# Matrix products that read and write in runs of 32 columns, alternating between the two halves of their columns

## The chip, the cores and the metric

The kernel runs on one NeuronCore of a Trainium2 chip. The metric is device time in microseconds (us) of one execution, start to end, and the time of a kernel is the median of several executions. Besides the times there is one profiled execution of the kernel before, from which all rows below are taken.

## What is computed

One block of a bidirectional encoder on 512 tokens of width 2048, in float32. A normed input is projected to 10,304 columns, which feed two attention branches of eight heads each: a differential one (two softmaxes, subtracted) and one with compressed queries, keys and values. Both are gated and merged, and one more product and a norm end the block. Cut to what matters:

```python
h = _rmsnorm(x, norm_g[layer])
proj = h @ w_in[layer]
aq, ak, av, ag, cq, ckv, kr, bg, mg = jnp.split(proj, SPLIT_POINTS, axis=-1)
...
oa = _diff_attention(aq[..., 0, :], aq[..., 1, :], ak[..., 0, :], ak[..., 1, :], av, pos_f, lam, slopes)
oa = _rmsnorm(oa, a_subln_g[layer], SUBLN_EPS) * (1.0 - lam_init)
ya = (oa.reshape(b, s, A_WIDTH) * jax.nn.silu(ag)) @ w_oa[layer]

q = (_rmsnorm(cq, q_norm_g[layer]) @ w_uq[layer]).reshape(b, s, B_HEADS, B_NOPE + B_ROPE)
kv = (_rmsnorm(ckv, kv_norm_g[layer]) @ w_ukv[layer]).reshape(b, s, B_HEADS, B_NOPE + B_V_DIM)
...
ob = _mla_attention(q_nope, q_rope, k_nope, k_rope, vb)
yb = (ob.reshape(b, s, B_WIDTH) * jax.nn.silu(bg)) @ w_ob[layer]

ga, gb = jnp.split(mg, 2, axis=-1)
merged = jax.nn.sigmoid(ga) * ya + jax.nn.sigmoid(gb) * yb
x = x + merged @ w_out[layer]
return _rmsnorm(x, final_g)
```

## The kernel before

**Numbers in two parts.** Every float32 operand of a large product is split into a high part, rounded to the format `float32r`, and a low part that holds the rest. `three` (L2113) makes one product of two such operands out of three TensorE instructions into the same bank of PSUM: high by high, high by low, low by high. Each of these instructions has a stationary operand of 128 x 128 words, loaded by a LDWEIGHTS of its own, and a moving operand of 128 partitions by 512 columns (256 columns in `pv`, L2183). Its result is 128 partitions by as many columns, and fills a whole bank of PSUM (2 KB in each partition) or half of one.

**Stages.** The program on TensorE is one stream, written out by hand. It begins with `WARM_UP` products of the identity and the transposes of the normed input (`turn_unit`, L2200). Then come 92 merge steps and what belongs to them (`merge_product`, L2289): the compressed columns, the values and the merge gates, the last two with Strassen's seven products in place of eight (`product`, L2236, with its sums `s12` and `s34`). Then eight heads of the first branch (`a_head`, L2426, with `project`, `scores_a`, `turn_p_a`, `pv` and `feature_sums`), eight of the second (`b_up`, `b_gate`, `scores_b`), the two products of the branches (`y_block`, L2582), and the last product (`merge_product` again, and a loop over `three` at the end, L2645 to L2660). `rotary_keys` (L2463) has products with a result of 64 partitions among its own.

**Operands.** Where a moving operand is a weight of a merge step, `hi_of` and `lo_of` hand it over as two blocks of 256 columns, `[P, 2, 256]`. In most steps the two blocks lie side by side, so that the instruction reads 512 words in one piece. In the steps whose raw data went into one of the two shared slots (`st.raw >= OWN_RAW`, in `blocks`, L478) the low part lies in the upper halves of rows of another tile, and the two blocks are 512 words apart: the instruction reads 256 words, jumps, and reads 256 more. The names `duo<-h_hi,s_hi`, `duo<-h_lo,s_hi`, `duo<-h_lo,h_hi` and `duo<-h_hi` at L2116 in the rows below are these steps; the first name after the arrow is the moving operand. All other moving operands and all results are one piece of consecutive words:

```python
own = o_hi[st.hi] if st.n >= OUT0 else m_hi[:, st.hi, :]
return own[:, p0 * SEQ:p1 * SEQ].rearrange("p (a b) -> p a b", b=HALF_T)
```

**Other engines.** ScalarE rounds the high parts, VectorE subtracts to get the low ones, SyncE starts the loads, and both compute engines read the banks when a group of products is complete. `duo` is the name of PSUM in the rows: four tensors of two banks each.

Of the kernel before, what the change touches and what calls it, by code (L numbers as in the profile page):

```python
# [27 lines left out]
KT = D_MODEL // P  # L28
# [8 lines left out]
LAM_INIT = 0.8 - 0.6 * math.exp(-0.3 * 0)  # L37
SLOPE0, SLOPE_RATIO = 2.0 ** (-8.0 / HEADS), 2.0 ** (-8.0 / HEADS)
NORM_EPS, SUBLN_EPS = 1e-6, 1e-5


SLOTS = 4
# [186 lines left out]
def hybrid_encoder(nc, x, positions, norm_g, w_in, lam_q1, lam_k1, lam_q2, lam_k2, a_subln_g, w_oa,  # L229
                   q_norm_g, w_uq, kv_norm_g, w_ukv, w_ob, w_out, final_g, consts, out):  # L230
    ctx = ExitStack()
    with ctx:
# [3 lines left out]
        def at(name, kb, shape, dt=F32):  # L236
            return nc.alloc_sbuf_tensor_at(name, shape, dt, offset=base + int(kb * KB))

        def sem(name):
            return ctx.enter_context(nc.semaphore(name))  # L240


        h_hi = at("h_hi", 0, [P, KT, SEQ], F32R)
        h_lo = at("h_lo", 32, [P, KT, SEQ], F32R)
# [62 lines left out]
        start = at("start", 96, [P, TOK, SEQ])  # L307
# [6 lines left out]
        q_hl = at("q_hl", 160, [P, 2, SEQ], F32R)  # L314
        k_hl = at("k_hl", 164, [P, 2, SEQ], F32R)


        qa = at("qa", 160, [P, 2, SEQ], F32R)
        ka = at("ka", 164, [P, 2, SEQ], F32R)
        ka_lo = at("ka_lo", 198, [P, 2, SEQ], F32R)  # L320
        vT = at("vT", 168, [P, SEQ])
        vT_lo = at("vT_lo", 168, [P, SEQ], F32R)
        vT_hi = at("vT_hi", 142, [P, SEQ], F32R)
# [12 lines left out]
        kr_hi = at("kr_hi", 198, [P, SEQ], F32R)  # L336
        kr_lo = at("kr_lo", 200, [P, SEQ], F32R)
        qr_hl = at("qr_hl", 202, [P, SEQ], F32R)
        v_raw = at("v_raw", 202, [P, TOK, P])
        ones_sq = at("ones_sq", 204, [P, P], F32R)  # L340
# [47 lines left out]
        ACC = bank[0:2]  # L388
        SC = bank[2:6]
        TR = bank[6]  # L390
# [44 lines left out]
        scored = sem("scored")  # L435
# [30 lines left out]
        LOW, HIGH = slice(0, 64), slice(64, P)  # L466
# [8 lines left out]
        def tile_no(head, t):  # L475
            return head * TOK + (t + 1)
# [11 lines left out]
        def lo_of(st, p0, p1):  # L488
            if st.n >= OUT0:
                return blocks(o_lo, mg_hi, mg_lo, st, p0, p1)  # L490
            return blocks(m_lo, h_hi, h_lo, st, p0, p1)

        def hi_of(st, p0, p1):
            own = o_hi[st.hi] if st.n >= OUT0 else m_hi[:, st.hi, :]
            return own[:, p0 * SEQ:p1 * SEQ].rearrange("p (a b) -> p a b", b=HALF_T)
# [1614 lines left out]

        @block.tensor
        def _(pe):
            def three(dst, lhs_hi, lhs_lo, rhs_hi, rhs_lo, start, stop):  # L2113

                pe.matmul(dst, lhs_hi, rhs_hi, start=start, stop=False)  # L2115
                pe.matmul(dst, lhs_hi, rhs_lo, start=False, stop=False)  # L2116
                return pe.matmul(dst, lhs_lo, rhs_hi, start=False, stop=stop)  # L2117

            def tile(piece, c0, width=P):
                return w_hi[:, piece.slot, c0:c0 + width], w_lo[:, piece.slot, c0:c0 + width]  # L2120
# [1 line left out]
            def project(piece, dst, half, halves, rhs_hi, rhs_lo, k0, midway=None):  # L2122

                pe.wait_ge(lo_ready, piece.after(0))
                for k in range(8):
                    if k == 4 and midway:
                        midway()
                    hi, lo = tile(piece, k * P)
                    last = three(dst[:, :], hi, lo, rhs_hi[:, k0 + k, :], rhs_lo[:, k0 + k, :],
                                 half == 0 and k == 0, half == halves - 1 and k == 7)  # L2130
                last.then_inc(used, 1)

            def scores_a(head, t, first):
                if t == 0:
                    pe.wait_ge(acc_read, head * A_READS + 2)
                if not first or t >= 2:
                    pe.wait_ge(max_taken, tile_no(head, t) - 2)
                a, b = SC[2 * (t % 2)], SC[2 * (t % 2) + 1]
                q = slice(t * P, (t + 1) * P)
                for m, dst in enumerate((a, b)):  # L2140

                    pe.matmul(dst[:, :], qa[:, m, q], ka[:, m, :], start=True, stop=False)  # L2142
                for m, dst in enumerate((a, b)):

                    last = pe.matmul(dst[:, :], qa[:, m, q], ka_lo[:, m, :], start=False, stop=True)  # L2145
                last.then_inc(scored, 1)

            def scores_b(h, t, prev):
                H = h + BH
                if t == 0:  # L2150
                    pe.wait_ge(acc_read, h * B_READS + (B_READ0 + 3))
                    pe.wait_ge(rope_lo, h + 2)
                if prev:
                    pe.wait_ge(pt_lo_ready, tile_no(H, t) - TOK)
                elif t == 0:
                    pe.wait_ge(v_kept, TOK + VB_COPIES)
                q = slice(t * P, (t + 1) * P)
                dst = SC[t][:, :]
                pe.matmul(dst, q_hl[:, 0, q], k_hl[:, 0, :], start=True, stop=False)  # L2159
                pe.matmul(dst, q_hl[:, 0, q], k_hl[:, 1, :], start=False, stop=False)  # L2160
                pe.matmul(dst, q_hl[:, 1, q], k_hl[:, 0, :], start=False, stop=False)  # L2161

                pe.matmul(dst, qr_hl[:, q], kr_hi[:, :], start=False, stop=False)  # L2163
                pe.matmul(dst, qr_hl[:, q], kr_lo[:, :], start=False, stop=True).then_inc(scored, 1)  # L2164

            def turn(src, dst, done):
                for k in range(TOK):
# [15 lines left out]
            def pv(head, pair, in_a=False):  # L2183
                if in_a and pair == 0 and (not isinstance(head, int) or head > 0):
                    pe.wait_ge(o_copied, head)
                pe.wait_ge(pt_lo_ready, tile_no(head, 2 * pair + 1))
                pe.wait_ge(v_lo_ready, head + 1)
                for k in range(TOK):
                    last = three(OB[:, pair * 2 * P:(pair + 1) * 2 * P], v_hl[:, 0, k, :], v_hl[:, 1, k, :],
                                 pt[:, 0, k, :], pt[:, 1, k, :], k == 0, k == TOK - 1)  # L2190
                last.then_inc(pv_done, 1)

            def feature_sums(done):
                pe.matmul(TR[:, :], ones_sq[:, :], vT_hi[:, :], start=True, stop=False)
                pe.matmul(TR[:, :], ones_sq[:, :], vT_lo[:, :], start=False, stop=True).then_inc(done, 1)

            pe.wait_ge(cst_in, 16)
            pe.wait_ge(ones_set, 5)
# [195 lines left out]
            for n in range(N_MERGE):  # L2394
                st = MERGE[n]
                last = merge_product(n)
# [66 lines left out]
            def rotary_keys(s):  # L2463
                piece = Piece(C0 + s)
                pe.wait_ge(lo_ready, piece.after(0))
                for k in range(8):
                    if k == 4:
                        tail(2 * s)
                    kt = 8 * (s % 2) + k
                    both = w_hi[:, piece.slot, k * P:(k + 1) * P]  # L2470
                    high = w_hi[:, piece.slot, k * P:k * P + B_ROPE]
                    if kt == 0:
                        pe.matmul(ACC[1][:, :], both, h_hi[:, kt, :], start=True, stop=False)
                    last = pe.matmul(ACC[1][LOW, :], high, h_lo[:, kt, :], start=False, stop=False)
                    if kt:
                        last = pe.matmul(ACC[1][:, :], both, h_hi[:, kt, :], start=False, stop=kt == KT - 1)
                last.then_inc(used, 1)

            def tail(q):
                if q < 2 * A_STEPS:  # L2480
                    a_extras(q, HEADS, False, True)
                for i in range(2 * LT):
                    if C_TURN_AT[i] == q:
                        turn_c(i)
# [97 lines left out]
            def y_block(u, i, t, halves):  # L2582
                branch = Y_UNITS[u][1]
                g_hi, g_lo = (ga_hi, ga_lo) if branch == 0 else (gb_hl[:, :, 0, :], gb_hl[:, :, 1, :])
                q = slice(t * P, (t + 1) * P)
                for k in range(2):
                    hi, lo = tile(Piece(Y0 + U_STEPS * u + i), k * SEQ, SEQ)
                    kt = 2 * i + k
                    last = three(y_bank(u, t)[:, :], g_hi[:, kt, q], g_lo[:, kt, q], hi, lo, kt == 0, kt == HEADS - 1)
                if i == U_STEPS - 1 and t < TOK - 1:  # L2590
                    last.then_inc(y_done, 1)
                return last
# [9 lines left out]
            for s in range(U_STEPS):  # L2602
                pe.wait_ge(ga_lo_ready, s + 1)
                for i in (2 * (s % 2), 2 * (s % 2) + 1):
                    pe.wait_ge(lo_ready, Piece(Y0 + i).after(0))
                    for t in (2 * (s // 2), 2 * (s // 2) + 1):
# [4 lines left out]
                        last = y_block(0, i, t, 2)  # L2611
# [7 lines left out]
            for s in range(U_STEPS, Y_STEPS):  # L2619
# [4 lines left out]
                for t in range(TOK):  # L2624
# [9 lines left out]
                    last = y_block(u, i, t, 4)  # L2634
# [10 lines left out]
            for t in range(TOK):  # L2645
                q = slice(t * P, (t + 1) * P)
# [5 lines left out]
                for n in range(MID_END, N_ALL):  # L2652
# [3 lines left out]
                    for j in range(4):  # L2656
                        kt = 4 * st.k + j
                        last = three(bank[L_BANK[t]][:, :], mg_hi[:, kt, q], mg_lo[:, kt, q], hi_of(st, j, j + 1),
                                     lo_of(st, j, j + 1), kt == 0, kt == KT - 1)
# [31 lines left out]
```

## Time and profile before

| | |
|---|---|
| time, median of 3 executions | 1429.8 us (1429.46 to 1430.91) |
| time of the profiled execution | 1429.3 us |
| its span, first to last instruction | 1427.5 us |
| granted TensorE clock, mean of the span | 0.999 of full speed |
| TensorE, matmul rows | 1413.2 us busy, 6604 instructions |
| TensorE, weight loads | 1175.1 us busy, 6604 instructions |
| VectorE | 1020.0 us busy |
| ScalarE | 707.1 us busy |

The span leaves out 1.8 us of the device time. Matmuls overlap one another in the profile: a row of 512 columns lasts 0.39 us, but the next one starts long before it has ended. What a product costs is therefore read from the distance of one start to the next, which is called its pace here, and not from the length of its row.

### The profile page before, as it was taken

What the parts mean: (1) busy time and instruction counts of PE and PEld (TensorE: products, weight loads), DVE (VectorE), ACT (ScalarE), POOL (GpSimd) and SP (SyncE); (2) the same over time, 40 slices, a digit from 0 to 9 for tenths busy, and PEclk for the clock granted to TensorE, in tenths of its full rate; (3) what the DMA queues carried; (4) which work ended last, traced back from release to release, by engine and by line L of the source; (5) the groups of instructions that cost most, each with busy time, mean ns of one, the idle gap of its engine ahead of it and who ended that gap; (6) DMA issues with size and microseconds to landing.
All of it is one profiled execution on the core that took longest, in us unless ns stands there. A gap on an engine that the chain in (4) does not pass through costs nothing.

```text
span 1427.5 us, 17881 instructions
## 1 busy us (share of the span) xinstructions
PE 1413.2 (99%) x6604; PEld 1175.1 (82%) x6604; DVE 1020.0 (71%) x1381; ACT 707.1 (50%) x894; POOL 31.5 (2%) x52
## 2 busy tenths in 40 slices
PE   8999999999999999999999999999999999999997
PEld 7888888888888888888888878888888888888886
DVE  6967898798878868677667656666676353478966
ACT  6546334544344456665666667555564222324434
POOL 0000000000000000000000000000000000000000
PEclk9999999999999999999999999999999999999999
DMA  8439576766756543222222434322242444617674
GB/s 300 145 125 316 177 263 186 236 213 212 238 184 207 184 146 83 79 82 81 81 81 82 114 106 133 84 72 66 81 140 74 151 125 152 207 45 247 197 254 172
DMA packets 182976, 218.43 MB, mean 153 GB/s; under 512 B 19456, under 2 KB 133248, under 8 KB 182272
## 3 DMA queue, kind: packets, MB, share of 16 engines
q1 hardware_dynamic: 174304, 197.64, 44.5%
q10 hardware_dynamic: 8608, 19.93, 3.6%
q8 instruction: 41, 0.67, 0.2%
q14 instruction: 23, 0.19, 0.0%
HBM read 195.51 MB, written 22.02 MB: 152 GB/s over the span
## 4 chain that ended last, share of the span: by engine, by line
PE 91%; DVE 3%; DMA 1%; ACT 1%; issue 1%; SPq 1%; POOL 0%; DVEq 0%; POOLq 0%; ACTq 0%
PE duo L2115 28%; PE duo L2117 28%; PE duo L2116 28%; PE duo L2168 2%; DMA start_y<-start_columns 1%; PE duo L2142 1%; PE duo L2145 1%; SPq L610 1%; ACT m_hi L886 1%; PE duo L2159 1%; PE duo L2164 1%; PE duo L2163 1%; PE duo L2160 1%; PE duo L2161 1%; PE duo L2598 0%
## 5 line engine op out<-in xcount | busy, mean ns | idle before, releaser
L1385 DVE TENSOR_TENSOR w_lo<-w_raw,w_hi 128x1024 fp32r<-128x1024 f32 (+1 forms) x116 | 135.3, 1167 | 99.3 <-ACT w_hi L781 98.7
L2115 PE MATMUL duo<-h_hi,w_hi 128*128 128x512 f32 x512 | 201.8, 394 | 0.0
L2117 PE MATMUL duo<-h_hi,w_lo 128*128 128x512 f32 x512 | 199.6, 390 | 0.0
L2116 PE MATMUL duo<-h_lo,w_hi 128*128 128x512 f32 x512 | 199.6, 390 | 0.0
L886 ACT ACTIVATE m_hi<-m_raw 128x2048 fp32r<-128x2048 f32 (+1 forms) x66 | 115.5, 1752 | 144.6 <-PE duo L2117 71.5
L781 ACT ACTIVATE w_hi<-w_raw 128x1024 fp32r<-128x1024 f32 (+1 forms) x118 | 119.2, 1011 | 124.3 <-DMA w_raw<-in_w_ob_dram 65.8
L1502 DVE TENSOR_TENSOR m_lo<-m_raw,m_hi 128x2048 fp32r<-128x2048 f32 (+3 forms) x71 | 141.9, 2001 | 26.9 <-ACT m_hi L886 26.5
L2115 PE MATMUL duo<-m_hi,h_hi 128*128 128x512 f32 x368 | 144.6, 393 | 1.6 <-DVE h_lo L1538 0.9
L2117 PE MATMUL duo<-m_hi,h_lo 128*128 128x512 f32 x368 | 143.3, 389 | 0.0
L2115 PE MATMUL duo<-m_hi,s_hi 128*128 128x512 f32 x320 | 124.5, 389 | 0.0
L2117 PE MATMUL duo<-m_hi,s_lo 128*128 128x512 f32 x320 | 124.5, 389 | 0.0
L2116 PE MATMUL duo<-m_lo,h_hi 128*128 128x512 f32 x300 | 116.8, 389 | 0.0
L2117 PEld LDWEIGHTS duo<-h_hi,w_lo 128*128 128x128 f32 x512 | 96.1, 188 | 20.6
L2116 PEld LDWEIGHTS duo<-h_lo,w_hi 128*128 128x128 f32 x512 | 96.3, 188 | 18.7
L2115 PEld LDWEIGHTS duo<-h_hi,w_hi 128*128 128x128 f32 x512 | 96.2, 188 | 18.7
L2116 PE MATMUL duo<-m_lo,s_hi 128*128 128x512 f32 x224 | 87.1, 389 | 0.0
L2115 PEld LDWEIGHTS duo<-m_hi,h_hi 128*128 128x128 f32 x368 | 69.1, 188 | 19.3 <-DVE m_lo L1502 2.4
L2117 PEld LDWEIGHTS duo<-m_hi,h_lo 128*128 128x128 f32 x368 | 69.1, 188 | 14.5
L1396 DVE TENSOR_TENSOR pt<-duo,pt 128x512 fp32r<-128x512 f32 x64 | 42.7, 687 | 45.7 <-ACT pt L794 45.5
L801 ACT ACTIVATE e<-e,small 128x512 f32<-128x512 f32 x64 | 45.8, 716 | 50.0 <-DVE small L1416 50.0
L2117 PEld LDWEIGHTS duo<-m_hi,s_lo 128*128 128x128 f32 x320 | 60.1, 188 | 12.5
L794 ACT ACTIVATE pt<-duo 128x512 fp32r<-128x512 f32 x64 | 36.3, 595 | 68.7 <-PE duo L2168 67.0
(322 smaller groups left out, 2991.0 us busy)
## 6 DMA issues: line engine op xcount, KB each, us to landing
m_raw<-in_w_in_dram SPq DMA_DIRECT2D x110, 512.0 KB, 4.7
w_raw<-in_w_in_dram SPq DMA_DIRECT2D x132, 256.0 KB, 3.0
o_raw<-in_w_out_dram SPq DMA_DIRECT2D x32, 512.0 KB, 5.1
spare<-in_w_in_dram SPq DMA_DIRECT2D x17, 512.0 KB, 4.6
h_raw<-in_w_in_dram SPq DMA_DIRECT2D x17, 512.0 KB, 4.9
w_raw<-in_w_oa_dram SPq DMA_DIRECT2D x32, 256.0 KB, 3.3
sig<-gates SPq DMA_DIRECT2D x8, 1024.0 KB, 6.3
w_raw<-in_w_ob_dram SPq DMA_DIRECT2D x32, 256.0 KB, 3.4
```

The lines of the kernel that those rows point to most:

```text
L610: sp.dma_start(dst, src).then_inc(m_in[st.raw], 16)
L781: act.activation(w_hi[:, piece.slot, 0:cols], w_raw[:, piece.slot, 0:cols], ACT.Copy).then_inc(hi_ready, 1)
L794: act.activation(pt[:, 0, :, (t % 2) * P:(t % 2 + 1) * P], src[:, :].rearrange("p (k c) -> p k c", k=TOK), ACT.Copy).then_inc(pt_hi_ready, 1)
L801: last = act.activation(e[:, t % 2, m, :], e[:, t % 2, m, :], ACT.Exp, bias=nm[:, b:b + 1], scale=A_SCALE, accum_out=sums[:, b:b + 1])
L886: act.activation(hi_of(st, 0, st.parts), raw_of(st, 0, st.parts), ACT.Copy).then_inc(m_hi_ready, 1)
L1385: dve.tensor_tensor(w_lo[:, piece.slot, 0:cols], w_raw[:, piece.slot, 0:cols], w_hi[:, piece.slot, 0:cols].bitcast(F32), ALU.subtract).the ...
L1396: dve.tensor_tensor(pt[:, 1, :, c], src[:, :].rearrange("p (k c) -> p k c", k=TOK), pt[:, 0, :, c].bitcast(F32), ALU.subtract).then_inc(pt ...
L1502: dve.tensor_tensor(lo_of(st, p0, p1), raw_of(st, p0, p1), hi_of(st, p0, p1).bitcast(F32), ALU.subtract).then_inc(done, 1)
L2115: pe.matmul(dst, lhs_hi, rhs_hi, start=start, stop=False)
L2116: pe.matmul(dst, lhs_hi, rhs_lo, start=False, stop=False)
L2117: return pe.matmul(dst, lhs_lo, rhs_hi, start=False, stop=stop)
L2168: last = pe.transpose(dst[:, k * P:(k + 1) * P], src[:, k * P:(k + 1) * P], ident)
```

## The change

All products of 512 or 256 columns go through a new function, `multiply`. It hands the moving operand and the bank to TensorE in another order of columns: a run of 32 columns of the first half, then the run of 32 of the second half, then the next of the first, and so on. Both sides have the same order, so each result lands in the place where it was. A product of 512 columns has 16 runs and 15 jumps between them, on either side; one of 256 columns has 8 runs and 7 jumps. The number of instructions, their order on every engine, the waits and the transfers stay as they are; in the built program the operands of a product are 128x8x2x32 where they were 128x512, and 128x4x2x32 where they were 128x256. Stationary operands, transposes and the first products of the identity are not touched.

```diff
+RUN = 32
...
         def _(pe):
+            def by_turns(columns):
+                if len(columns.shape) == 3:
+                    return columns.rearrange("p j (c r) -> p c j r", r=RUN)
+                return columns.rearrange("p (j c r) -> p c j r", j=2, r=RUN)
+
+            def multiply(dst, lhs, rhs, start, stop):
+                return pe.matmul(by_turns(dst), lhs, by_turns(rhs), start=start, stop=stop)
+
             def three(dst, lhs_hi, lhs_lo, rhs_hi, rhs_lo, start, stop):
 
-                pe.matmul(dst, lhs_hi, rhs_hi, start=start, stop=False)
-                pe.matmul(dst, lhs_hi, rhs_lo, start=False, stop=False)
-                return pe.matmul(dst, lhs_lo, rhs_hi, start=False, stop=stop)
+                multiply(dst, lhs_hi, rhs_hi, start=start, stop=False)
+                multiply(dst, lhs_hi, rhs_lo, start=False, stop=False)
+                return multiply(dst, lhs_lo, rhs_hi, start=False, stop=stop)
...
-                    pe.matmul(dst[:, :], qa[:, m, q], ka[:, m, :], start=True, stop=False)
+                    multiply(dst[:, :], qa[:, m, q], ka[:, m, :], start=True, stop=False)
```

The same replacement of `pe.matmul` by `multiply` stands in the rest of `scores_a`, in `scores_b`, `feature_sums` and `rotary_keys`.

## Rows read from the trace of the kernel before

**Rows 1.** The page, busy time, share and instructions of each engine.

```profile
PE 1413.2 (99%) x6604; PEld 1175.1 (82%) x6604; DVE 1020.0 (71%) x1381; ACT 707.1 (50%) x894; POOL 31.5 (2%) x52
```

**Rows 2.** The page, busy tenths and granted clock in 40 slices.

```profile
PE   8999999999999999999999999999999999999997
...
DVE  6967898798878868677667656666676353478966
...
PEclk9999999999999999999999999999999999999999
```

**Rows 3.** The page, the chain that ended last, by engine and line.

```profile
PE 91%; DVE 3%; DMA 1%; ACT 1%; issue 1%; SPq 1%; POOL 0%; DVEq 0%; POOLq 0%; ACTq 0%
PE duo L2115 28%; PE duo L2117 28%; PE duo L2116 28%; PE duo L2168 2%; DMA start_y<-start_columns 1%; PE duo L2142 1%; PE duo L2145 1%; SPq L610 1%; ACT m_hi L886 1%; PE duo L2159 1%; PE duo L2164 1%; PE duo L2163 1%; PE duo L2160 1%; PE duo L2161 1%; PE duo L2598 0%
```

**Rows 4.** TensorE's groups by shape: busy us, mean ns, idle before.

```profile
L2115 PE MATMUL duo<-pt,v_hl 128*128 128x256 f32 x128 | 36.8, 288 | 1.6 <-DVE pt L1396 1.6
...
L2168 PE MATMUL duo<-cst,e 128*128 128x128 f32 x128 | 19.5, 275 | 0.1
...
L2221 PE MATMUL duo<-cst 128*128 128x128 f32 x4 | 0.6, 275 | 0.0
```

**Rows 5.** TensorE in order of time, the last loop: start us, length us, instruction.

```profile
1376.15 0.39 PE L2115 MATMUL duo<-o_hi,mg_hi 128*128 128x512 f32 x1
...
1419.44 0.39 PE L2117 MATMUL duo<-o_hi,mg_lo 128*128 128x512 f32 x1
```

**Rows 6.** The same view, the ends of a stretch of merge steps.

```profile
299.84 0.50 PE L2115 MATMUL duo<-m_hi,h_hi 128*128 128x512 f32 x1
300.17 0.39 PE L2116 MATMUL duo<-h_lo,h_hi 128*128 128x512 f32 x1
...
301.33 0.39 PE L2115 MATMUL duo<-m_hi,h_hi 128*128 128x512 f32 x1
...
375.00 0.39 PE L2116 MATMUL duo<-m_lo,s_hi 128*128 128x512 f32 x1
```

**Rows 7.** That stretch by windows: us, TensorE busy (instructions), clock, DMA share, GB/s.

```profile
300.00:375.00 75.00, 75.00 (x332) 1.00 0.70 223
```

**Rows 8.** The groups by shape within that stretch that read two pieces.

```profile
L2116 PE MATMUL duo<-h_lo,s_hi 128*128 128x512 f32 x12 | 4.7, 389 | 0.0
L2116 PE MATMUL duo<-h_lo,h_hi 128*128 128x512 f32 x10 | 3.9, 390 | 0.0
L2116 PE MATMUL duo<-h_hi,s_hi 128*128 128x512 f32 x8 | 3.1, 389 | 0.0
L2116 PE MATMUL duo<-h_hi 128*128 128x512 f32 x6 | 2.3, 389 | 0.0
```

**Rows 9.** In order of time, scores of a head that change banks.

```profile
559.91 0.62 PE L2142 MATMUL duo<-ka,qa 128*128 128x512 f32 x2
560.37 0.61 PE L2145 MATMUL duo<-ka_lo,qa 128*128 128x512 f32 x2
560.82 0.39 PE L2115 MATMUL duo<-h_hi,w_hi 128*128 128x512 f32 x1
```

**Rows 10.** In order of time, twelve products of 256 columns and what follows.

```profile
636.09 0.28 PE L2115 MATMUL duo<-pt,v_hl 128*128 128x256 f32 x1
...
637.52 0.40 PE L2115 MATMUL duo<-h_hi,w_hi 128*128 128x512 f32 x1
637.76 0.40 PE L2116 MATMUL duo<-h_lo,w_hi 128*128 128x512 f32 x1
...
638.46 0.39 PE L2116 MATMUL duo<-h_lo,w_hi 128*128 128x512 f32 x1
```

**Rows 11.** In order of time, all engines: the last transfer's start.

```profile
1423.42 0.41 SPq L730 DMA_DIRECT2D out_dram<-start  x1
```

More of the change, by code:

```diff
@@ L2140, in scores_a @@
                 for m, dst in enumerate((a, b)):
-                    pe.matmul(dst[:, :], qa[:, m, q], ka[:, m, :], start=True, stop=False)
+                    multiply(dst[:, :], qa[:, m, q], ka[:, m, :], start=True, stop=False)
                 for m, dst in enumerate((a, b)):
-                    last = pe.matmul(dst[:, :], qa[:, m, q], ka_lo[:, m, :], start=False, stop=True)
+                    last = multiply(dst[:, :], qa[:, m, q], ka_lo[:, m, :], start=False, stop=True)
                 last.then_inc(scored, 1)
@@ L2158, in scores_b @@
                 dst = SC[t][:, :]
[L2159 to L2164, printed above, removed]
+                multiply(dst, q_hl[:, 0, q], k_hl[:, 0, :], start=True, stop=False)
+                multiply(dst, q_hl[:, 0, q], k_hl[:, 1, :], start=False, stop=False)
+                multiply(dst, q_hl[:, 1, q], k_hl[:, 0, :], start=False, stop=False)
+                multiply(dst, qr_hl[:, q], kr_hi[:, :], start=False, stop=False)
+                multiply(dst, qr_hl[:, q], kr_lo[:, :], start=False, stop=True).then_inc(scored, 1)
             def turn(src, dst, done):
@@ L2193, in feature_sums @@
             def feature_sums(done):
-                pe.matmul(TR[:, :], ones_sq[:, :], vT_hi[:, :], start=True, stop=False)
-                pe.matmul(TR[:, :], ones_sq[:, :], vT_lo[:, :], start=False, stop=True).then_inc(done, 1)
+                multiply(TR[:, :], ones_sq[:, :], vT_hi[:, :], start=True, stop=False)
+                multiply(TR[:, :], ones_sq[:, :], vT_lo[:, :], start=False, stop=True).then_inc(done, 1)
             pe.wait_ge(cst_in, 16)
@@ L2472, in rotary_keys @@
                     if kt == 0:
-                        pe.matmul(ACC[1][:, :], both, h_hi[:, kt, :], start=True, stop=False)
-                    last = pe.matmul(ACC[1][LOW, :], high, h_lo[:, kt, :], start=False, stop=False)
+                        multiply(ACC[1][:, :], both, h_hi[:, kt, :], start=True, stop=False)
+                    last = multiply(ACC[1][LOW, :], high, h_lo[:, kt, :], start=False, stop=False)
                     if kt:
-                        last = pe.matmul(ACC[1][:, :], both, h_hi[:, kt, :], start=False, stop=kt == KT - 1)
+                        last = multiply(ACC[1][:, :], both, h_hi[:, kt, :], start=False, stop=kt == KT - 1)
                 last.then_inc(used, 1)
```

## The prediction, made before the changed kernel ran

> **What bounds the kernel now.** I read the page's busy times first, then its slices, then the chain, and after that single stretches in order of time. TensorE is busy for 1413.2 of 1427.5 us [rows 1], with nine tenths or more in all slices but the first and the last, at full granted clock throughout [rows 2]: its upper level, 2.4 GHz. Rows of matmuls overlap, so 99% alone proves little; the chain does, since 91% of it is TensorE, and 84% the three lines of `three` [rows 3]. VectorE, the next busiest, has 71% over the span, though nine tenths in a few slices of the merge steps [rows 1, 2]. So the time is the number of products times their pace, and the whole question is what the pace of a product does when its words come in 16 runs.
>
> The pace before is very even. The last loop has 4 token blocks x 4 steps x 4 tiles x 3 = 192 products of 512 columns. From the start of the first to that of the last are 43.29 us, or 191 paces of 226.65 ns [rows 5]. Twelve products of 256 columns take 637.52 - 636.09 = 1.43 us, 119.2 ns each [rows 10]. Through these two goes the line (226.65 - 119.17) / 256 = 0.420 ns a column, and 226.65 - 512 x 0.420 = 11.7 ns a product that do not depend on its columns. At 2.4 GHz a period is 0.417 ns, so the columns themselves already run at about one a period. The pace doesn't ask which bank is written: where the scores of a head go from one bank to another and back, four products take 560.82 - 559.91 = 0.91 us, 227.5 ns each, which is the same within the 10 ns to which starts are printed [rows 9].
>
> **The change part by part.** No instruction, wait or transfer is added or taken away, so nothing on VectorE, ScalarE or SyncE has a cost of its own. TensorE has 6604 instructions [rows 1]; 460 of them have 128 columns and stay as they are, seven groups of the view by shape, of which the first and the last are shown [rows 4]; 3 x 128 = 384 have 256 columns, of which one line of three is shown [rows 4]. That leaves 5760 of 512. Each gets 15 jumps in what it reads and 15 in what it writes; the 384 get 7 and 7.
>
> *Jumps on the reading side.* The trace of before has such products: those of the shared slots read two pieces. From 300.17 to 375.00 us are 330 paces (332 instructions in the window, the first of which is the one at 299.84) [rows 6, 7], and 36 of these products read two pieces [rows 8]. The first five follow a pause and are a little long; from 301.33 on are 325 paces in 73.67 us, 226.68 ns each, with 34 jumps in them. At 226.65 ns they would take 73.66 us, so that the jumps cost 0.009 us together, 0.3 ns each, and with the printed hundredths of the four starts against me at most 0.9 ns. Less than nothing is not excluded by as much. Between these ends I take zero: 0.3 ns would be a part of a period, and is what rounding makes. The upper end would be 15 x 0.9 = 13.5 ns a product, 5760 x 13.5 = 78 us, and 384 x 7 x 0.9 = 2 us more: +80 us.
>
> *Jumps on the writing side.* No row of before has a result in more than one piece, so that this is the real unknown. The nearest rows are those of the reading side, with the same bounds, 0 to 0.9 ns a jump. I take zero here too: a run of 32 words, aligned to 32, leaves every smaller group of words together, and the even pace across a change of bank [rows 9] says that a result may go on at another address without a stall. That a bank's two halves have a price or a gain in alternation, nothing shows.
>
> *The fixed 11.7 ns.* If these hang on the order in which words are read and written, the change could touch them. All of them would be 6144 x 11.7 = 72 us. Against it: they are there after a change of bank and within one bank, with one piece and with two [rows 6 to 9], and just as well at 256 columns, which were used to find them. I take that they stay.
>
> So the sum is 1429.3 us (the profiled execution: 1427.5 and 1.8 around it) + 0 + 0 + 0. The profiled execution lies 0.5 us under the median of the runs; for that I forecast **1429.8 us**, no change. The end of the kernel is no cover for anything: the last product starts at 1419.44 and the last transfer follows 4 us later [rows 5, 11], whatever the pace is.
>
> **The rivals.**
>
> *A. The jumps cost something: slower.* In its mildest form that is one period of 0.417 ns per jump, on the writing or the reading side: 15 x 0.417 = 6.25 ns a product, 5760 x 6.25 + 384 x 7 x 0.417 = 37 us, so 1467 us. It is slower than the 0.2% that a measurement can tell from no change (2.9 us) from 0.03 ns a jump on. For it speaks that nothing in the trace writes in pieces; against it the 34 jumps on the reading side. The upper end of their bound would give 1510 us.
>
> The Trainium skill speaks for this rival: "PSUM — Partial Sum Buffer", in its Specifications, says of the 8-byte lines of PSUM that any pattern that isn't contiguous slows matmuls significantly. No run here shows a write in pieces. "Advanced Engine Details and Errata", under PSUM Cachelines, narrows the same rule to every two consecutive words being side by side, and by that the runs of this change cost nothing. I hold to the narrower wording, since the reading side has a rule of the same kind and its jumps show no cost here.
>
> *B. The products fall out of their even pace: slower.* The pace can be worse without any pause: after products of 256 columns, the next four of 512 take 638.46 - 637.52 = 0.94 us, 235 ns each, 8.35 ns over the even pace [rows 10]. If jumps kept TensorE in that state, 5760 x 8.35 = 48 us would come on top: 1478 us. Against it: the state is gone within a few products, also in steps that read two pieces [rows 6].
>
> *C. The alternation frees something: faster.* If one half of a bank or of an operand rests while the other is used, and the 11.7 ns are the price of not resting, up to 72 us go: 1358 us. Half of that would be 1394 us. VectorE would take it in nearly all stages, with its 71% [rows 1], though not in the few slices of nine tenths [rows 2]. For it speaks that these 11.7 ns are lost in each product and that nothing in the trace says to what. Against it: the loss is per product and not per column, while the alternation acts on every column.
>
> The Trainium skill would have less lost: "TensorE: Matmul & The Clock Gate", under Back-to-back issue gap, gives N / 2.4 + 2.5 ns, 215.8 ns for 512 columns. The rows here say 226.65, and the measurement decides; were the page's pace reached, an estimate would be 5760 x 10.8 = 62 us less, about 1367 us.
>
> *D. The change doesn't do what it says.* The built program could have joined the runs again; but alternating runs can't be joined, and its operands stand as 128x8x2x32. This would give 1429.8 us as well and has no chance of its own.
>
> **How the numbers follow.** The forecast, no change within 0.2%, gets 0.56: every row that bears on it agrees, but the writing side is dark. A gets 0.15, B 0.07, C 0.22, of which a good third for half of its price or less. Faster is 0.22 (C), same 0.56, slower 0.22 (A and B). For the range I take in the mild form of A and all of B, up to 1478 us, and the lesser half of C, down to 1394 us, rounded to 1392. Left out are the greater half of C (0.13) and the dear end of A (0.04). The likeliest case alone has a range of 1427 to 1432.7 us.
>
> **What would show it.** In the profile after, the start-to-start distance of the last loop's 192 products decides: 226.6 ns is the forecast; 232.9 ns or more is A, and then the pace at 256 columns should grow by half as much, 7 jumps to 15; around 235 ns everywhere, with an uneven distance from one product to the next, is B; 215 ns, and 107.5 ns at 256 columns, is C with all of its price. In the forecast the chain stays with TensorE at 91%, and VectorE, ScalarE and the transfers keep their times to the microsecond. I would be wrong in kind if a run of 32 words has a beginning or an end that TensorE or PSUM has to pay for, or if the two halves of a bank or of a row of words work apart from each other: the rows of before can't tell either, because nothing in them writes in pieces and nothing reads in more than two.

## The result, and the profile after

The changed kernel takes 1479.64 us (median of 4, 1479.47 to 1480.01) against 1429.63 us for the kernel before (1429.28 to 1430.91): a ratio of 1.0349, with a 95% interval of 1.0331 to 1.0366. It is slower, by 50 us, and 1.6 us beyond the upper end of the range.

The page after, busy time by engine and then the chain that ended last:

```profile
PE 1464.3 (99%) x6604; PEld 1183.9 (80%) x6604; DVE 1020.4 (69%) x1381; ACT 706.7 (48%) x894; POOL 31.7 (2%) x52
...
PE 94%; DVE 2%; DMA 1%; issue 1%; SPq 1%; ACT 1%; POOL 0%; DVEq 0%; POOLq 0%
PE duo L2122 91%; PE duo L2179 2%; DMA start_y<-start_columns 1%; SPq L613 1%; PE duo L2609 0%; DMA m_raw<-in_w_in_dram 0%; DVE mid L2084 0%; DVE mid L2077 0%; PE duo L2215 0%; ACT e L804 0%; DVE c_lo L1853 0%; DVE e L1413 0%; DVE start L2081 0%; DVE w_lo L1388 0%; DVE m_lo L1505 0%
```

Against [rows 1] TensorE has 51.1 us more with the same 6604 instructions, and VectorE and ScalarE have what they had, to within 0.4 us. The chain is TensorE's still, more than in [rows 3]. The last loop after, first and last of its 192 products (start us, length us, instruction):

```profile
1424.56 0.40 PE L2122 MATMUL duo<-o_hi,mg_hi 128*128 128x512 f32 x1
...
1469.76 0.40 PE L2122 MATMUL duo<-o_hi,mg_lo 128*128 128x512 f32 x1
```

That is 45.20 us, or 191 paces of 236.6 ns, where [rows 5] had 226.65: 10.0 ns more a product of 512 columns. The pace is not even any more. Five products in a row in a projection of the first branch:

```profile
564.36 0.40 PE L2122 MATMUL duo<-h_hi,w_lo 128*128 128x512 f32 x1
564.59 0.40 PE L2122 MATMUL duo<-h_hi,w_hi 128*128 128x512 f32 x1
564.83 0.40 PE L2122 MATMUL duo<-h_lo,w_hi 128*128 128x512 f32 x1
565.07 0.40 PE L2122 MATMUL duo<-h_hi,w_lo 128*128 128x512 f32 x1
565.30 0.40 PE L2122 MATMUL duo<-h_hi,w_hi 128*128 128x512 f32 x1
```

In the trace's nanoseconds the paces of the last loop go from 233 to 241, where before they were 226 and 227. The products of 256 columns, on the other hand, are no slower. Twelve of them after, and the product that follows:

```profile
658.78 1.59 PE L2122 MATMUL duo<-pt,v_hl 128*128 128x256 f32 x12
660.21 0.40 PE L2122 MATMUL duo<-h_hi,w_hi 128*128 128x512 f32 x1
```

They take 1.43 us, as in [rows 10], with 7 jumps in each. So the whole change is in the products of 512. 5760 times 10.0 ns would be 57.6 us. Some 7 us are not seen: the products that follow shorter ones had an uneven pace before already [rows 10], and TensorE's longer stops, over 345 ns from one start to the next, came to 11.2 us before and to 6.2 us after, which fits other engines that do the same work in more time.

### The profile page after: what moved, and what is told of

Same layout as the page of the kernel before. It is cut to its first block, busy times and chain, and to the rows that moved or that the text cites. A ratio compares the mean times of both kernels' runs of the same rounds, so it can differ in the third digit from the quotient of the medians.

```text
span 1477.8 us, 17881 instructions
## 1 busy us (share of the span) xinstructions
PE 1464.3 (99%) x6604; PEld 1183.9 (80%) x6604; DVE 1020.4 (69%) x1381; ACT 706.7 (48%) x894; POOL 31.7 (2%) x52
## 4 chain that ended last, share of the span: by engine, by line
PE 94%; DVE 2%; DMA 1%; issue 1%; SPq 1%; ACT 1%; POOL 0%; DVEq 0%; POOLq 0%
PE duo L2122 91%; PE duo L2179 2%; DMA start_y<-start_columns 1%; SPq L613 1%; PE duo L2609 0%; DMA m_raw<-in_w_in_dram 0%; DVE mid L2084 0%; DVE mid L2077 0%; PE duo L2215 0%; ACT e L804 0%; DVE c_lo L1853 0%; DVE e L1413 0%; DVE start L2081 0%; DVE w_lo L1388 0%; DVE m_lo L1505 0%
## 5 line engine op out<-in xcount | busy, mean ns | idle before, releaser
L2122 PE MATMUL duo<-h_hi,w_hi 128*128 128x512 f32 x528 | 212.7, 403 | 0.0
L2122 PE MATMUL duo<-h_lo,w_hi 128*128 128x512 f32 (+1 forms) x528 | 210.9, 400 | 0.0
L2122 PE MATMUL duo<-h_hi,w_lo 128*128 128x512 f32 x512 | 204.5, 399 | 0.0
L2122 PE MATMUL duo<-m_hi,h_lo 128*128 128x512 f32 x368 | 146.9, 399 | 0.0
L2122 PE MATMUL duo<-m_hi,s_lo 128*128 128x512 f32 x320 | 127.8, 399 | 0.0
L2122 PE MATMUL duo<-m_hi,s_hi 128*128 128x512 f32 x320 | 127.8, 399 | 0.0
L2122 PEld LDWEIGHTS duo<-h_hi,w_hi 128*128 128x128 f32 x528 | 99.8, 189 | 23.6
L2122 PEld LDWEIGHTS duo<-h_lo,w_hi 128*128 128x128 f32 (+1 forms) x528 | 99.0, 188 | 23.0
L2122 PE MATMUL duo<-w_hi,gb_hl 128*128 128x512 f32 x256 | 82.4, 400 | 0.0
L2122 PEld LDWEIGHTS duo<-m_hi,s_hi 128*128 128x128 f32 x320 | 60.5, 189 | 15.2
```

Source lines behind the costliest of these rows:

```text
L2122: return pe.matmul(by_turns(dst), lhs, by_turns(rhs), start=start, stop=stop)
```

## The experiments

Each kernel ran once, with a profile, beside a run of the kernel before on the same chip (1429.4 to 1430.5 us). What decides is the pace. For 512 columns it is taken from the last loop, as above; where products have fewer columns or results, from the last 47 products of that loop, which have one shape but for the opening one left out (46 paces). The fences are TensorE in order of time, the first and the last of these products.

### Which side pays, and how long a run must be

Runs on the reading side only, `e1_read_runs`:

```diff
-                return pe.matmul(by_turns(dst), lhs, by_turns(rhs), start=start, stop=stop)
+                return pe.matmul(dst, lhs, by_turns(rhs), start=start, stop=stop)
```

> Only the moving words are read in alternating runs of 32; each bank is written in one piece, so that the columns of every product land in another order and the output is not the reference's. Measured so far: the pace of a product of 512 columns is 226.7 ns before and 236.7 ns with runs on both sides. Theory R (the reading side pays for its jumps): 236 to 237 ns, about 1480 us. Theory W (the writing side pays): 226.7 ns, about 1430 us. Theory S (TensorE loses an even pace as soon as anything in a product is broken up): 236 to 237 ns here and in the run with the writing side alone.

```profile
1424.33 0.40 PE L2122 MATMUL duo<-o_hi,mg_hi 128*128 128x512 f32 x1
...
1469.53 0.40 PE L2122 MATMUL duo<-o_hi,mg_lo 128*128 128x512 f32 x1
```

45.20 us, 236.6 ns; 1479.37 us in all, the time of the whole change.

Runs on the writing side only, `e2_write_runs`:

```diff
-                return pe.matmul(by_turns(dst), lhs, by_turns(rhs), start=start, stop=stop)
+                return pe.matmul(by_turns(dst), lhs, rhs, start=start, stop=stop)
```

> Only the banks are written in alternating runs of 32; the moving words are read in one piece (two in the shared slots), so that the columns of every product land in another order and the output is not the reference's. Theory R (reading pays): 226.7 ns a product, about 1430 us. Theory W (writing pays): 236 to 237 ns, about 1480 us. Theory S (an even pace is lost whichever side is broken up): 236 to 237 ns. If both sides pay a part, the two runs add up to 10 ns over the even pace.

```profile
1376.16 0.39 PE L2122 MATMUL duo<-o_hi,mg_hi 128*128 128x512 f32 x1
...
1419.45 0.39 PE L2122 MATMUL duo<-o_hi,mg_lo 128*128 128x512 f32 x1
```

43.29 us, 226.6 ns; 1429.28 us. The loss is the reading side's alone: theory R.

Runs of 64 and of 128 on both sides, `e3_run64` and `e4_run128`:

```diff
-RUN = 32
+RUN = 64
```

> Runs of 64 columns on both sides: 7 jumps in a product of 512 columns in place of 15. Theory J (each jump has a price, 10.0 ns / 15 = 0.67 ns): 226.7 + 4.7 = 231.3 ns, about 1453 us. Theory S (an even pace is lost, however many jumps): 236 to 237 ns, about 1480 us. Theory L (a run shorter than some length is what costs): 226.7 ns, about 1430 us, or 236 to 237 ns, with nothing between.

```profile
1377.42 0.39 PE L2122 MATMUL duo<-o_hi,mg_hi 128*128 128x512 f32 x1
...
1420.72 0.39 PE L2122 MATMUL duo<-o_hi,mg_lo 128*128 128x512 f32 x1
```

```diff
-RUN = 32
+RUN = 128
```

> Runs of 128 columns on both sides: 3 jumps in a product of 512 columns; the products of 256 columns are read and written in one piece. Theory J (a price per jump): 226.7 + 2.0 = 228.7 ns, about 1439 us. Theory S (an even pace is lost, however many jumps): 236 to 237 ns, about 1480 us. Theory L (short runs cost): 226.7 ns, about 1430 us.

```profile
1376.85 0.39 PE L2122 MATMUL duo<-o_hi,mg_hi 128*128 128x512 f32 x1
...
1420.14 0.39 PE L2122 MATMUL duo<-o_hi,mg_lo 128*128 128x512 f32 x1
```

43.30 and 43.29 us: 226.7 and 226.6 ns, 1430.54 and 1429.97 us. Seven jumps and three cost nothing. A price per jump falls (J), and so does the loss of an even pace by any jump (S). With the runs in this order there is a length between 32 and 64 words (128 and 256 bytes) from which on a run is free: theory L.

Runs of 16 on both sides, `e5_run16`:

```diff
-RUN = 32
+RUN = 16
```

> Runs of 16 columns on both sides: 31 jumps in a product of 512 columns. So far, by the reading side alone: 0, 1, 3 and 7 jumps 226.7 ns, 15 jumps 236.7 ns. Theory M (each jump of the reading side has a price of 3 to 3.7 periods of 0.417 ns, of which a product hides 32 periods, its fixed 13 ns): 512 + 31 x 3 to 3.7 periods, 252 to 261 ns a product, 1580 to 1630 us. Theory B (words come in blocks of 64, and each visit of a block takes at least 35.5 periods, however few of its words are wanted): 32 visits, 473 ns a product, about 2850 us.

```profile
1442.87 0.40 PE L2122 MATMUL duo<-o_hi,mg_hi 128*128 128x512 f32 x1
...
1488.71 0.40 PE L2122 MATMUL duo<-o_hi,mg_lo 128*128 128x512 f32 x1
```

45.84 us, 240.0 ns, and 1498.55 us. Both theories fall: M wanted 252 ns or more, B 473. Twice the jumps cost 3.4 ns more.

Every second run first, then the others, `e6_near_runs`:

```diff
-                return columns.rearrange("p (j c r) -> p c j r", j=2, r=RUN)
+                return columns.rearrange("p (c j r) -> p j c r", j=2, r=RUN)
```

> Runs of 32 columns on both sides, but every second run first and the others afterwards (0, 2, 4 to 14, then 1, 3 to 15): again 15 jumps, 14 of them over 32 words only in place of 256. The 200 products of the shared slots keep the order of the change. Theory M (a price per jump, whatever its distance): 236.7 ns a product, about 1480 us. Theory B (blocks of 64 words, each visited twice): the same 236.7 ns. Theory D (a jump between far places, as the two halves are, is what costs): 226.7 ns, about 1430 us.

```profile
1423.59 0.40 PE L2132 MATMUL duo<-o_hi,mg_hi 128*128 128x512 f32 x1
...
1468.79 0.40 PE L2132 MATMUL duo<-o_hi,mg_lo 128*128 128x512 f32 x1
```

45.20 us, 236.6 ns, 1478.66 us: the distance of a jump doesn't matter (D falls).

Neighbours exchanged, 1, 0, 3, 2, and so on, `e7_swapped_runs`:

```diff
-                return columns.rearrange("p (j c r) -> p c j r", j=2, r=RUN)
+                return columns.rearrange("p (c j r) -> p c j r", j=2, r=RUN)[:, :, ::-1, :]
```

> Runs of 32 columns on both sides in the order 1, 0, 3, 2, 5, 4 and so on: 15 jumps again, but both runs of every aligned 64 words (256 bytes) are read one after the other. The 200 products of the shared slots keep the order of the change. Theory M (a price per jump, whichever): 236.7 ns a product, about 1480 us. Theory B (blocks of 64 words, a visit has a least time): each block is visited once, 226.7 ns, about 1430 us.

```profile
1402.50 0.39 PE L2133 MATMUL duo<-o_hi,mg_hi 128*128 128x512 f32 x1
...
1446.88 0.40 PE L2133 MATMUL duo<-o_hi,mg_lo 128*128 128x512 f32 x1
```

44.38 us, 232.4 ns, 1456.72 us: as many jumps, about half the loss. Neither theory had that, and it gave the next one (K, below).

The writing side in runs of 2 words, `e8_write_runs_of_2`:

```diff
-RUN = 32
+RUN = 2
...
-                return pe.matmul(by_turns(dst), lhs, by_turns(rhs), start=start, stop=stop)
+                return pe.matmul(by_turns(dst), lhs, rhs, start=start, stop=stop)
```

> Only the banks are written out of order, in runs of 2 words (8 bytes), alternating between the halves: 255 jumps in a product of 512 columns; moving words are read as before, so that the columns of every product land in another order and the output is not the reference's. Theory F (the writing side is free as long as two words lie together): 226.7 ns a product, about 1430 us. Theory W2 (a jump of the writing side has a price too, hidden at 15 jumps): over 230 ns; at one period for each jump 512 + 255 periods, 320 ns, about 1965 us.

```profile
1378.05 0.39 PE L2122 MATMUL duo<-o_hi,mg_hi 128*128 128x512 f32 x1
...
1421.34 0.39 PE L2122 MATMUL duo<-o_hi,mg_lo 128*128 128x512 f32 x1
```

43.29 us, 226.6 ns, 1431.15 us: 255 jumps cost nothing on the writing side. The Trainium skill's wide wording in "PSUM — Partial Sum Buffer", Specifications (any pattern that isn't contiguous slows matmuls significantly), doesn't hold here; the narrower one that "Advanced Engine Details and Errata" adds under PSUM Cachelines (every two words side by side) agrees with these 0 ns.

Runs of 4 on both sides, `e12_run4`:

```diff
-RUN = 32
+RUN = 4
```

> Runs of 4 columns (16 bytes) on both sides, 127 jumps in a product of 512 columns. Runs of 16 take 576 periods, only 8 more than runs of 32. Theory Q (the loss is at its most where a run is 16 words or less): 576 periods, 240.0 ns, about 1499 us. Theory J2 (a jump has a small price of its own from some number on, half a period as between 31 and 15 jumps): 576 + 48 periods, 260 ns, about 1615 us; at one period each 672 periods, 280 ns, about 1730 us.

```profile
1500.31 0.41 PE L2122 MATMUL duo<-o_hi,mg_hi 128*128 128x512 f32 x1
...
1548.06 0.41 PE L2122 MATMUL duo<-o_hi,mg_lo 128*128 128x512 f32 x1
```

47.75 us, 250.0 ns, 1557.91 us. It is more than runs of 16 (Q falls) and less than J2 had, even at half a period a jump.

### What the loss hangs on

Weight loads of half the size, `e9_half_weights`:

```diff
+                if not start and not stop:
+                    dst, lhs = dst[0:P // 2], lhs[:, 0:P // 2]
```

> The order of the kernel before, but every product that neither opens nor closes its group has a stationary operand of 64 columns in place of 128, and so only the lower 64 partitions of a bank: half of each weight load and half of the results are left out, and the output is not the reference's. So far a product of 512 columns takes 544 periods of 0.417 ns in the order of before, 568 with runs of 32 and 576 with runs of 16, on the reading side alone. Theory C (the weight load that runs beside a product takes reads from it, 32 periods of it in the even pace): half a load takes 16, a product beside such a load 528 periods, 220.0 ns. Theory P (the reading of the moving words itself loses 1 period in every 16 words, whatever is loaded): 226.7 ns.

```profile
1421.74 0.40 PE L2119 MATMUL duo<-o_lo,mg_hi 128*64 128x512 f32 x1
...
1432.33 0.39 PE L2119 MATMUL duo<-o_hi,mg_lo 128*128 128x512 f32 x1
```

10.59 us for 46 paces, 230.2 ns; 1442.16 us. Both fall: half a load is not cheaper to have beside a product (C; its row is 134 ns long, where a whole one has 188), and yet the load is not indifferent (P), for the pace is worse than with a whole one, and uneven (224 to 236 ns). The edit halves what each product writes as well, so this run alone doesn't show that it is the load.

384 columns in one piece, `e10_cols384`, and in runs of 16 on the reading side, `e11_cols384_read_runs16`; the second has, besides, the words by turns of the halves with `r=16`:

```diff
+                if not start and dst.shape[1] == SEQ:
+                    dst = dst[:, 0:384]
+                    rhs = rhs[:, :, 0:192] if len(rhs.shape) == 3 else rhs[:, 0:384]
```

> The order of the kernel before, but every product of 512 columns that doesn't open its group has 384 columns: a quarter of its result is left out, and the output is not the reference's. Theory P (1 period lost in every 16 words): 384 x 17/16 = 408 periods, 170.0 ns. Theory C (32 periods lost to each weight load): 416 periods, 173.3 ns.

```profile
1238.57 0.34 PE L2120 MATMUL duo<-o_lo,mg_hi 128*128 128x384 f32 x1
...
1246.55 0.34 PE L2120 MATMUL duo<-o_hi,mg_lo 128*128 128x384 f32 x1
```

> As the run before it, 384 columns in place of 512 in every product that doesn't open its group, with the output not the reference's; but the words are read in alternating runs of 16 (banks are written in one piece). Theory P (2 periods lost in every 16 words): 384 x 18/16 = 432 periods, 180.0 ns. Theory C (64 periods lost to each weight load): 448 periods, 186.7 ns.

```profile
1245.33 0.34 PE L2123 MATMUL duo<-o_lo,mg_hi 128*128 128x384 f32 x1
...
1253.61 0.34 PE L2123 MATMUL duo<-o_hi,mg_lo 128*128 128x384 f32 x1
```

7.98 us, 173.5 ns in one piece; 8.28 us, 180.0 ns in runs of 16. So in one piece the loss is per product, as C has it (512 columns lose 13.3 ns against one column a period of 0.417 ns, 384 lose 13.5), and in runs of 16 it is per column, as P has it: 180.0 / 384 and 240.0 / 512 are both 0.469 ns. Neither theory alone stands.

What fits all of this qualitatively is theory K, which is on record with the next runs: places within 64 words come round in turn, the moving read and the read of the next weights go through them side by side, and collide according to their phase. That the two are side by side shows in the rows of all kernels; here the changed one, a product and the weight load that begins with it (PEld is the row of the load):

```profile
1469.05 0.40 PE L2122 MATMUL duo<-o_hi,mg_lo 128*128 128x512 f32 x1
1469.06 0.19 PEld L2122 LDWEIGHTS duo<-o_hi,mg_hi 128*128 128x128 f32 x1
```

Runs of 64 leave the order of places alone, and so does a jump between two pieces 512 words apart. The order 1, 0, 3, 2 shifts it by half a turn. The other runs break it up. Why 64 words: runs of 64 in alternation from two far places cost nothing, runs of 32 in the same alternation do. The test: shift the start and keep one piece (`f1_offset32`, `f2_offset16`, `f3_offset48`, with `g2_cols448` as their unshifted reference), or make jumps that keep the order (`f4_turning_runs`). To have room, all products but the opening ones have 448 columns:

```diff
+                if not start and dst.shape[1] == SEQ:
+                    dst = dst[:, 0:448]
...
+                        rhs = rhs[:, 32:480]
```

> The order of the kernel before, one piece, but products that don't open their group have 448 columns, and read them from the 33rd word of their 512 on (a start 128 bytes further); a part of the computation is left out and the output is not the reference's. From 512 and 384 columns, at an even pace of columns + 32 periods, 448 columns take 480 periods, 200.0 ns, if the start doesn't matter. Theory K (the words of a partition lie in parts that take turns within 64 words; the reading of the moving words and that of the next weights collide when both want the same part, and the order of the parts decides how often): the start changes the phase of the two, as the order 1, 0, 3, 2 did, so about 5.7 ns more, 206 ns, and uneven. Theory T (a run under 64 words has a price of its own): 200.0 ns, even.

```profile
1311.47 0.36 PE L2124 MATMUL duo<-o_lo,mg_hi 128*128 128x448 f32 x1
...
1320.85 0.36 PE L2124 MATMUL duo<-o_hi,mg_lo 128*128 128x448 f32 x1
```

With `rhs[:, 16:464]` and `rhs[:, 48:496]` in its place:

> As the run before it, 448 columns with the output not the reference's, but read from the 17th word on (64 bytes further). Theory K: another phase, so another pace than 200.0 ns, above or below it. Theory T: 200.0 ns, even.

```profile
1302.00 0.37 PE L2124 MATMUL duo<-o_lo,mg_hi 128*128 128x448 f32 x1
...
1311.20 0.37 PE L2124 MATMUL duo<-o_hi,mg_lo 128*128 128x448 f32 x1
```

> As the two runs before it, 448 columns with the output not the reference's, but read from the 49th word on (192 bytes further). Theory K: another phase again, so another pace than 200.0 ns, above or below it. Theory T: 200.0 ns, even.

```profile
1306.58 0.36 PE L2124 MATMUL duo<-o_lo,mg_hi 128*128 128x448 f32 x1
...
1315.88 0.37 PE L2124 MATMUL duo<-o_hi,mg_lo 128*128 128x448 f32 x1
```

And with `rhs[:, 0:448]`:

> The order of the kernel before, 448 columns from the first word on in every product that doesn't open its group, with the output not the reference's: the reference for the three shifted starts and for the turning runs, which gave 203.8, 200.1, 202.2 and 204.0 ns a product. From 512 and 384 columns (columns + 32 periods): 480 periods, 200.0 ns and even, under theories K and T alike. If it is as uneven as the others and over 202 ns, a start doesn't matter and 448 columns are out of step by themselves.

```profile
1312.83 0.37 PE L2124 MATMUL duo<-o_lo,mg_hi 128*128 128x448 f32 x1
...
1322.33 0.37 PE L2124 MATMUL duo<-o_hi,mg_lo 128*128 128x448 f32 x1
```

The reference takes 9.50 us, 206.5 ns; the 200.0 ns that I had worked out for it were wrong. It is not uneven here: after the first three, all paces are 206 or 207 ns, which is columns + 48 periods where 512 and 384 columns have columns + 32. Against it the three shifts give 9.38, 9.20 and 9.30 us: 203.9, 200.0 and 202.2 ns, all three uneven. In this loop the start alone, by 64 bytes, changes the pace by 6.5 ns. Under T nothing could. So 448 columns leave the expected pace by themselves, but a start does matter.

Two limits belong to this. K wanted 5.7 ns more for the shift by 32 words, and it was 2.6 ns less. And at 448 columns the last loop is not the whole kernel: over all products of 448 columns whose next start comes within 250 ns, the trace has 204.0 ns for the reference and for `f4_turning_runs` below, and 203.6, 200.7 and 202.5 ns for the three shifts. The order is the same, the differences are about half or less: 64 bytes are 3.3 ns there, and 10.0 us of the kernel's time (1333.58 to 1323.62 us), while the shift by 32 words is 0.4 ns and 1.1 us, no more than runs of one kernel differ. In `f3_offset48` the products of the shared slots, which the last loop doesn't contain, read from the 33rd word.

Runs of 32 in the order 0, 3, 2, 5, 4, 7 to 12, 15:

```diff
+                        rhs = bass.AP(rhs.tensor, rhs.offset, [list(rhs.ap[0]), [64, 7], [96, 2], [1, 32]])
```

> 448 columns in every product that doesn't open its group, with the output not the reference's, read in 14 runs of 32 in the order 0, 3, 2, 5, 4, 7 to 12, 15: 13 jumps, but even and odd runs take turns as in one piece, so that places within 64 words come round as in one piece and with the same start. The 200 products of the shared slots read two pieces of 224. Theory K (only the order of places within 64 words counts): as one piece, 480 periods, 200.0 ns, even. Theory T (a run under 64 words costs, wherever it goes): 71/64 of 448, 497 periods, 207 ns.

```profile
1313.00 0.37 PE L2124 MATMUL duo<-o_lo,mg_hi 128*128 128x448 f32 x1
...
1322.50 0.37 PE L2124 MATMUL duo<-o_hi,mg_lo 128*128 128x448 f32 x1
```

9.50 us, 206.5 ns: exactly the reference in one piece, and in the trace's nanoseconds the 46 paces are the same one by one. At 448 columns thirteen jumps and runs of 128 bytes cost nothing, if places within 64 words come round as they do in one piece. T's 207 ns are met in number only, since the reference has no short runs and takes as long. At 512 columns this order was not tried.

The last test leaves moving words and banks as they were, at 512 columns, and shifts only the weights, `g1_weights_offset32`:

```diff
+                row = lhs.ap[0][0]
+                if not start and lhs.shape[1] == P and row >= 2 * P:
+                    by = 32 if lhs.offset % (2 * P) == 0 else -32
+                    lhs = bass.AP(lhs.tensor, lhs.offset + by, [list(d) for d in lhs.ap])
```

> Moving words and banks as in the kernel before, 512 columns in one piece; but every product that doesn't open its group loads its 128 x 128 stationary words from 32 columns (128 bytes) further along, or from 32 columns before where that would leave the tile, so that the weights are the wrong ones and the output is not the reference's. The order of work and its amount are unchanged. Theory K (the moving read and the weight read beside it collide, by which place within 64 words each is at): the phase is shifted as in the run that read from the 33rd word, so an uneven pace some 4 to 6 ns over 226.7 ns, about 1450 to 1460 us. Theory M1 (only the moving read's own start and order count, not the weights): 226.7 ns, even, about 1430 us.

```profile
1403.06 0.40 PE L2121 MATMUL duo<-o_hi,mg_hi 128*128 128x512 f32 x1
...
1447.43 0.40 PE L2121 MATMUL duo<-o_hi,mg_lo 128*128 128x512 f32 x1
```

44.37 us, 232.3 ns, uneven (227 to 241), and 1457.26 us. Not one moving word is read from another place or in another order, and the kernel is 28 us slower: M1 falls, K stands. A load that is slower by itself because it begins elsewhere is not the reason, as far as the rows show it. One group of loads before and in this run, by line and shape (count, busy us, mean ns, idle before):

```profile
L2117 PEld LDWEIGHTS duo<-h_hi,w_lo 128*128 128x128 f32 x512 | 96.1, 188 | 20.6
...
L2121 PEld LDWEIGHTS duo<-h_hi,w_lo 128*128 128x128 f32 x512 | 96.4, 188 | 22.7
```

Both take 188 ns, begin with a product and are over some 36 and 41 ns before the next one starts. The pace is that of `e7_swapped_runs` (232.4 ns), where the order of the moving words was shifted by as much and the weights were not. This fits K, by which what counts is how the two lie to each other. The run that would show it, both shifted together, which by K brings back 226.7 ns, was not made.

The Trainium skill has it otherwise: "TensorE: Matmul & The Clock Gate", Step-by-step, says that the moving operand and the weight load have read ports of their own, so that loading the next weights takes nothing from the running product. These 5.7 ns for a shift of the weights by 128 bytes disagree with the latter, and the measurement decides; of the ports themselves they say nothing.

**What is shown and what isn't.** Shown: the loss is on the reading side; it is no price of a jump or of its distance; the pace depends on the order in which places within 64 words (256 bytes) of a partition are read, and, with the moving read unchanged, on where the weights begin that are loaded beside it; jumps that keep the order are free. Argued, not shown: that the two reads collide, and how. Theory K doesn't give the sizes: why runs of 16 lose per column, why runs of 4 lose another 10 ns, why 448 columns leave the pace of columns + 32 periods that 512 and 384 keep, and why the products of 256 columns, read in the same order as those of 512, lose nothing. No faster kernel came of it. At 448 columns a start 64 bytes further won 6.5 ns a product in the last loop, but from a reference that loses more than 512 columns do; a shift by 16 or 48 words at 512 columns was not tried.

## Why the prediction was wrong

**The bound by TensorE, and what costs nothing elsewhere**: right. VectorE, ScalarE and the number of instructions are unchanged, and 50 of the 57.6 us that the pace costs show in the end.

**Jumps on the reading side, the step that failed.** I took 0 ns from the 34 products that read two pieces, with a bound of 0.9 ns a jump [rows 6 to 8]. The reading of the rows was right, but the rows don't bear on this change: their jump, from one 256-word block to another 512 words on, comes after a multiple of 64 words and goes over a multiple of 64, so that it leaves the order of places alone. `e3_run64` has seven such jumps and loses nothing. I treated a jump as the thing that costs, where the order of places within 64 words was what had changed. The term measured 10.0 ns a product; as a price per jump it would be 0.67 ns, within my bound of 0.9, but there is no such price. (The bound itself is a little low: with the loop's rounding carried from 191 paces to 325 it is 1.1 ns a jump. Nothing hangs on it.)

**Jumps on the writing side**: zero, as I took it; the "real unknown" was none. `e2_write_runs` and `e8_write_runs_of_2` settle it where the reading is in one piece, the latter for 255 jumps.

**The fixed 11.7 ns**: they stayed, as forecast, where 512 or 384 columns are read in one aligned piece. `e10_cols384` gives 173.5 ns, and the line through 256 and 512 columns 226.65 - 128 x 0.420 = 172.9. They are no constant, though: at 448 columns the line has 199.8 ns, and `g2_cols448` took 206.5.

**The rivals.** A had the right sign and the wrong mechanism: the pace at 256 columns should have risen, and it stood still. B was nearest. I named 235 ns, uneven, and 1478 us; it was 236.6 ns, from 233 to 241, and 1479.6 us. An even pace does give way to a lasting uneven one; whether it is the state that one sees for a few products after shorter ones [rows 10], no run shows. That the number came so near is in part luck: the starts in [rows 10] are printed to 10 ns, and in the trace's nanoseconds those four products take 232.5 ns each, which would have made 34 us of B's 48. I gave it 0.07 and no reason, since I had the state down as what a pause or a jump leaves behind, when the runs point to a phase between two reads; and I put its price at the end of the range without room above, which is why the time lies 1.6 us outside. No row of before could price an order or a phase: by the places of the kernel's tiles all moving and stationary operands began at multiples of 64 words and were read upwards. C didn't happen.

## What to carry to other kernels

An even pace over thousands of products shows that a state is kept, not that it can't be lost: before a pattern of addresses is changed, ask which property all operands have in common, here their alignment to 256 bytes, since no row can price what never varied. For float32r products of 512 columns, keep the moving operand in runs of at least 64 words that begin at multiples of 64, with the weights aligned alike. That is no rule for every width: at 448 columns the aligned start was the slowest of the four that ran. Writing a bank in alternation, down to runs of two words, cost nothing while the reading was in one piece. When a whole change costs a few per cent, halve it by side first: two runs, one for reads and one for writes, said more here than all sums.

## What was not expected of the hardware

Shifting the weights by 128 bytes, with moving words and banks as they were, made 512-column products 5.7 ns slower (226.6 to 232.3 ns) and the kernel 28 us. Halving the weight loads, and with them the results, made them 3.6 ns slower (230.2 ns). Writing a bank in 256 runs of 2 words cost nothing (226.6 ns). And in the last loop a product of 448 columns took 206.5 ns from the first word on, but 200.0 ns from the 17th (204.0 and 200.7 ns over the whole kernel).
